# Delta-rule tiles of a two-block transformer in compact form: two 64-token chunks' diagonal blocks side by side, 64x64 products on quarters of the array

## The reference, cut to what matters

```
kb = k * beta[..., None]
lower = jnp.where(strict, jnp.einsum('bhncd,bhnsd->bhncs', kb, k) * decay, 0.0)
rhs = jnp.concatenate([v * beta[..., None], kb * jnp.exp(g)[..., None]], axis=-1)
sol = lax.linalg.triangular_solve(jnp.eye(C, dtype=jnp.float32) + lower, rhs,
                                  left_side=True, lower=True, unit_diagonal=True)
u, wk = sol[..., :Dv], sol[..., Dv:]
intra = jnp.where(incl, jnp.einsum('bhncd,bhnsd->bhncs', q, k) * decay, 0.0)
def step(S, inp):
    qc, kc, uc, wc, gc, ac = inp
    v_new = uc - jnp.einsum('bhck,bhkv->bhcv', wc, S)
    o = jnp.einsum('bhck,bhkv->bhcv', qc * jnp.exp(gc)[..., None], S) + jnp.einsum('bhcs,bhsv->bhcv', ac, v_new)
    S = S * jnp.exp(g_last)[..., None, None] + jnp.einsum(
        'bhck,bhcv->bhkv', kc * jnp.exp(g_last[..., None] - gc)[..., None], v_new)
```

## Time and profile before

| | us |
|---|---|
| median of 3 runs | 4289.7 (4287.04 to 4289.97) |
| the profiled execution | 4289.53 |
| its span in the trace | 4287.6 |
| PE, DVE, ACT, POOL busy | 3966.6, 1481.8, 1432.2, 1341.2 |
| mean granted TensorE clock | 0.935 of full speed |

### The profile page before, as it was taken

The page is one execution under the profiler, slowest core; times in us unless marked ns, Lnnn a source line. Parts: engine busy times, 40 slices in busy tenths (PEclk is TensorE's granted clock), DMA queues, the critical chain, the costliest instruction groups (busy, mean ns, idle before and its releaser), DMA issues.

```text
span 4287.6 us, 49148 instructions
## 1 busy us (share of the span) xinstructions
PE 3966.6 (93%) x20324; PEld 3286.1 (77%) x20324; DVE 1481.8 (35%) x3082; ACT 1432.2 (33%) x2399; POOL 1341.2 (31%) x639
## 2 busy tenths in 40 slices
PE   8988999998899979999988889999999998879999
PEld 7776888877688868877677778887887757778887
DVE  2344111334411231225855531112112686653111
ACT  2543222344322242234442232223223453313221
POOL 3203443410344444433200034443443320003443
PEclk9988999998899989999888899999999988889999
DMA  4102333210233333322100023333233210003232
GB/s 117 40 20 64 91 101 99 72 45 15 71 95 96 108 83 93 98 88 71 35 1 1 1 84 92 100 96 92 91 101 89 68 32 1 1 3 92 91 101 89
DMA packets 406767, 292.31 MB, mean 68 GB/s; under 512 B 18032, under 2 KB 356880, under 8 KB 406544
## 3 DMA queue, kind: packets, MB, share of 16 engines
q1 hardware_dynamic: 400976, 284.96, 22.4%
q10 hardware_dynamic: 5136, 2.96, 0.3%
q0 software_dynamic: 432, 1.25, 0.1%
HBM read 287.03 MB, written 2.10 MB: 67 GB/s over the span
## 4 chain that ended last, share of the span: by engine, by line
PE 54%; DVE 7%; ACT 2%; issue 1%; POOL 0%; ACTq 0%; DMA 0%; DVEq 0%; SPq 0%
PE ps L687 8%; PE ps L689 8%; PE ps L688 8%; PE ps L743 5%; PE ps L745 5%; PE ps L744 5%; PE ps L1264 1%; PE ps L1252 1%; PE ps L1271 1%; PE ps L789 1%; PE ps L1043 1%; PE ps L806 1%; DVE mix L1478 1%; PE ps L797 1%; PE ps L1354 1%
## 5 line engine op out<-in xcount | busy, mean ns | idle before, releaser
L2810 POOL TENSOR_TENSOR wl<-wraw,wh 128x1024 fp32r<-128x1024 f32 (+2 forms) x532 | 1248.0, 2347 | 2408.7 <-ACT wh L2242 2408.6
L687 PE MATMUL ps<-x_T,wh 128*128 128x512 f32 (+1 forms) x2672 | 1029.9, 385 | 33.4 <-DVE x_T L1443 23.7
L688 PE MATMUL ps<-x_T,wh 128*128 128x512 f32 (+1 forms) x2672 | 1022.6, 383 | 0.0
L689 PE MATMUL ps<-x_T,wl 128*128 128x512 f32 (+1 forms) x2672 | 1022.1, 383 | 0.0
L2242 ACT ACTIVATE wh<-wraw 128x1024 fp32r<-128x1024 f32 (+2 forms) x532 | 548.8, 1033 | 1149.7 <-PE ps L745 644.2
L687 PEld LDWEIGHTS ps<-x_T,wh 128*128 128x128 f32 x2672 | 512.1, 192 | 144.4 <-issue 48.4
L689 PEld LDWEIGHTS ps<-x_T,wl 128*128 128x128 f32 x2672 | 511.5, 191 | 95.9
L688 PEld LDWEIGHTS ps<-x_T,wh 128*128 128x128 f32 x2672 | 512.2, 192 | 93.8 <-issue 0.5
L743 PE MATMUL ps<-wh,h_T 128*128 128x512 f32 x1056 | 417.6, 395 | 27.4 <-issue 27.4
L745 PE MATMUL ps<-wh,h_T 128*128 128x512 f32 x1056 | 415.9, 394 | 0.0
L744 PE MATMUL ps<-wl,h_T 128*128 128x512 f32 x1056 | 415.8, 394 | 0.0
(11 more groups left out here) (812 smaller groups left out, 5214.8 us busy)
## 6 DMA issues: line engine op xcount, KB each, us to landing
wraw<-in_ffn_w_gate_dram SPq DMA_DIRECT2D x88, 512.0 KB, 3.8
wraw<-in_ffn_w_up_dram SPq DMA_DIRECT2D x88, 512.0 KB, 3.9
wraw<-in_w_in_dram SPq DMA_DIRECT2D x82, 512.0 KB, 3.8
wraw<-in_ffn_w_down_dram SPq DMA_DIRECT2D x80, 512.0 KB, 3.7
wraw<-in_w_gate_dram SPq DMA_DIRECT2D x44, 512.0 KB, 3.9
wraw<-in_w_up_dram SPq DMA_DIRECT2D x44, 512.0 KB, 3.9
wraw<-in_w_down_dram SPq DMA_DIRECT2D x40, 512.0 KB, 3.7
wraw<-in_w_o_dram SPq DMA_DIRECT2D x16, 512.0 KB, 3.4
```

The source lines that it names most:

```text
L687: mm(b[:, t0:t1], wh[:, k, :], xTh[:, k, t0:t1], k == 0, False)
L688: mm(b[:, t0:t1], wh[:, k, :], xTl[:, k, t0:t1], False, False)
L689: ins = mm(b[:, t0:t1], wl[:, k, :], xTh[:, k, t0:t1], False, k == 7)
L2810: tt(wl, raw_of(w), wh.bitcast(F32), ALU.subtract).then_inc(*g.sig("w", "lo", w))
```

## The change

Only the chunks' own 64x64 blocks are kept. The block of tokens 0 to 63 stands in partitions 0 to 63, the block of tokens 64 to 127 in partitions 64 to 127, over the same 64 columns. Four heads take 128x256, and both halves g share a buffer of 128x512: `Dm`, `Dt`, `N`, `Yk`. The products on them are 64x64x64, one for each chunk: the first reads rows 0 to 63 and writes PSUM partitions 0 to 63, the second rows 64 to 127 to partitions 64 to 127, of the same bank. The output is split: `od` holds what needs no state and is copied by ACT; the state's part `o` is added to Y by DVE. The masks become 64 columns wide.

```diff
+                def each(b, g, lhs, rhs):
+                    for h in range(4):
+                        for c in HALF:
+                            hs = slice(g * 256 + h * 64, g * 256 + h * 64 + 64)
+                            ins = mm(b[c, h * 64:(h + 1) * 64], lhs[c, hs], rhs[c, hs], True, True)
+                    return ins
...
-                        for h in range(4):
-                            hs = slice(h * P, (h + 1) * P)
-                            ins = mm(b[:, hs], N_[:, hs], D_[:, hs], True, True)
-                        ins.then_inc(*S("y", k, g))
+                        each(b, g, N, Dm).then_inc(*S("y", k, g))
...
-                    mm(b[:, 0:256], F2[hb(h), p_ * P:(p_ + 1) * P], fa, True, True)
-                    mm(b[:, 256:512], F2[hb(h), 256 + p_ * P:384 + p_ * P], fa, True,
-                       True).then_inc(*S("rw", h))
+                    for q in range(2):
+                        for n in range(2):
+                            for e_, c in enumerate(HALF):
+                                o = q * 256 + n * P
+                                ins = mm(b[c, o:o + P].rearrange("p (c n) -> p c n", c=2),
+                                         F2[rs, n * 256 + q * P + 64 * e_:n * 256 + q * P + 64 * e_ + 64],
+                                         f1v[rs, q, :, c], True, True)
...
-                for h in range(8):
-                    ins = mm(b[hb(h), (h // 2) * P:(h // 2 + 1) * P], KB[:, h * 64:(h + 1) * 64],
-                             (DR if h < 4 else DG)[:, (h % 4) * P:(h % 4 + 1) * P], True, True)
-                ins.then_inc(*S("wt"))
+                for e_, c in enumerate(HALF):
+                    b, free = bank(K("wt", e_), K("WT", e_))
+                    pe.wait_ge(*free)
+                    for h in range(8):
+                        ins = mm(b[hb(h), (h // 2) * 64:(h // 2 + 1) * 64], KB[c, h * 64:(h + 1) * 64],
+                                 Dm[c, h * 64:(h + 1) * 64], True, True)
+                    ins.then_inc(*S("wt", e_))
...
+                    ins.then_inc(*S("ubx", par))
...
-                        pe.wait_ge(*at(*K("WT")))
+                        pe.wait_ge(*at(*K("ubx", par)))
+                        pe.wait_ge(*at(*K("WT", e_)))
...
-                        if h < 4:
-                            mm(o, RW[h][:, 0:128], un, True, False)
-                            mm(o, RW[h][:, 256:384], VV[:, h * 64:(h + 1) * 64], False, False)
-                        else:
-                            mm(o, PN[par][:, (q - 2) * 256:(q - 2) * 256 + 128], un, True, False)
+                    for c in HALF:
+                        if h < 4:
+                            mm(b[c, hs], RW[h % 2][c, o:o + 64], UN[c, us], True, False)
+                        else:
+                            ins = mm(b[c, hs], PN[c, (h - 4) * P:(h - 4) * P + 64], UN[c, us], True, True)
...
-                        v.copy_predicated(v4(D_), lvm(k, 0).bitcast(I32), v4(psum_of(*K("d", k, g))[:, :])).then_inc(
-                            *S("D", k, g))
+                        v.copy_predicated(v4(D_), lvm(k, 0).bitcast(I32),
+                                          v4(psum_of(*K("d", k, g))[:, 0:256])).then_inc(*S("D", k, g))
...
-                for h in range(4):
-                    ins = tt(DR[:, h * P:(h + 1) * P], RW[h][:, 128:256], lvl(0), ALU.mult)
+                for par in range(2):
+                    ins = tt(Dm[:, 0:256].rearrange("p (q r n) -> p q r n", q=2, r=2)[:, :, par, :],
+                             RW[par].rearrange("p (q c n) -> p q c n", q=2, c=4)[:, :, 1, :], lvm(0, 0, 2), ALU.mult)
...
-                v.wait_ge(*at(*K("Y", 1)))
+                v.wait_ge(*at(*K("Y")))
+                for par in range(2):
+                    yp = Y.rearrange("p (q r n) -> p q r n", q=4, r=2)[:, :, par, :]
+                    v.wait_ge(*at(*K("o", par)))
+                    step(tt(yp, yp, v4(psum_of(*K("o", par))[:, 0:256]), ALU.add), *K("Yo", par))
```

More of the change, by code:

```diff
@@ L66, in make_consts @@
     same = (r // 64) == (c // 64)
+    r64, c64 = r % 64, np.arange(64)[None, :]
     lv = []
-    for k in range(6):
-        w = 1 << k
-        m = ((r // (2 * w)) == (c // (2 * w))) & ((r // w) % 2 == 0) & ((c // w) % 2 == 1)
-        lv.append(m.astype(f))
-    for k in range(6):
-        lv.append(lv[k].T.copy())
+    for tr in range(2):
+        for k in range(6):
+            w = 1 << k
+            a, b = (c64, r64) if tr else (r64, c64)
+            lv.append((((a // (2 * w)) == (b // (2 * w))) & ((a // w) % 2 == 0) & ((b // w) % 2 == 1)).astype(f))
+    lv += [(r64 <= c64).astype(f), (r64 < c64).astype(f), (r64 > c64).astype(f), (r64 == c64).astype(f)]
     ind = np.stack([(i < 64), (i >= 64)], 1).astype(f)
     c2 = np.concatenate(common + [rope_tab(32), (same & (r <= c)).astype(f), (same & (r < c)).astype(f),
-                                  (same & (r > c)).astype(f), ind] + lv[8:], 1)
-    r1, r2 = np.concatenate(masks + swa, 1), np.concatenate(lv[:8], 1)
-    assert c1.shape[1] == N1 and c2.shape[1] == N2 and r1.shape[1] == N3
+                                  (same & (r > c)).astype(f), ind], 1)
+    r1, r2 = np.concatenate(masks + swa, 1), np.concatenate(lv, 1)
+    assert c1.shape[1] == N1 and r2.shape[1] == N3 - R_X and c2.shape[1] == N2 and r1.shape[1] == N3
     return [np.ascontiguousarray(c_.astype(f)) for c_ in (c1, c2, r1, r2)]
@@ L1261, in rec_tile @@
                         pe.wait_ge(*at(*K("Dt", k - 1, g)))
-                        for h in range(4):
-                            hs = slice(h * P, (h + 1) * P)
-                            ins = mm(b[:, hs], Dt_[:, hs], y_[:, hs], True, True)
-                        ins.then_inc(*S("d", k, g))
+                        each(b, g, Dt, Yk).then_inc(*S("d", k, g))
                         if k < 5:
@@ L1268, in rec_tile @@
                             pe.wait_ge(*free)
[L1269 to L1273 removed]
+                            each(b, g, Yk, Dt).then_inc(*S("dt", k, g))
+                        if g:
+                            stock.put(pe, l, Yk)
                         yield
[L1275 removed]
+                stock.put(pe, l, Dt, N)
                 yield SOLVED
@@ L1335, in rec_tile @@
                 Y = get()
+                b, free = bank(K("od"), K("Y"))
+                pe.wait_ge(*free)
+                for h in range(8):
+                    hs, us = slice(h * 64, (h + 1) * 64), slice((h % 2) * 256 + (h // 2) * 64, (h % 2) * 256 + (h // 2) * 64 + 64)
+                    o = (h // 2) * 256
+                    for c in HALF:
+                        if h < 4:
+                            mm(b[c, hs], RW[h % 2][c, o:o + 64], UN[c, us], True, False)
+                        else:
+                            ins = mm(b[c, hs], PN[c, (h - 4) * P:(h - 4) * P + 64], UN[c, us], True, True)
+                    if h < 4:
+                        for c in HALF:
+                            mm(b[c, hs], RW[h % 2][c, o + P:o + P + 64], VV[c, hs], False, True)
@@ L2035, in rec_tile @@
                 yield
[L2036 to L2038 removed]
+                DTN = get()
+                RW = [get(), get()]
+                DT, DN = DTN[:, 0:256], DTN[:, 256:512]
                 v.wait_ge(*at(*K("gd")))
[L2040 to L2043 removed]
@@ L2689, in rec_tile @@
                 copy(X[:, 0:256], psum_of(*K("x"))[:, 0:256]).then_inc(*S("X"))
-                s.wait_ge(*at(*K("wt")))
-                copy(WT, psum_of(*K("wt"))[:, :]).then_inc(*S("WT"))
+                for e_ in range(2):
+                    s.wait_ge(*at(*K("wt", e_)))
+                    copy(WT[:, e_ * 256:e_ * 256 + 256], psum_of(*K("wt", e_))[:, 0:256]).then_inc(*S("WT", e_))
                 yield
@@ L2701, in rec_tile @@
                 Y = get()
-                for par in range(2):
-                    s.wait_ge(*at(*K("o", par)))
-                    copy(Y.rearrange("p (q r n) -> p q r n", q=4, r=2)[:, :, par, :],
-                         psum_of(*K("o", par))[:, 0:256].rearrange("p (q n) -> p q n", q=4)).then_inc(*S("Y", par))
-                stock.put(s, l, *RW, *PN, DR, DG, X, WT, K2, F1, F3)
+                s.wait_ge(*at(*K("od")))
+                copy(Y, psum_of(*K("od"))[:, :]).then_inc(*S("Y"))
+                stock.put(s, l, *RW, PN, Dm, X, WT, K2, F1, F3)
                 yield PASSED
```

257 lines of the change are left out of this document (117 added, 140 removed).

## The result

| | before | after |
|---|---|---|
| median of 4 runs | 4288.4 (4282.5 to 4290.0) | 4139.0 (4134.1 to 4140.1) |
| the profiled execution, its span | 4289.5, 4287.6 | 4140.1, 4138.2 |
| PE, DVE busy | 3966.6, 1481.8 | 3826.4, 1392.1 |
| mean granted clock | 0.935 | 0.926 |

The ratio is 0.9652, 95% interval 0.9635 to 0.9669: 149 us less, where the forecast was 51 less (4238, range 4140 to 4310). It is the first rival's number, 4130, that came within 9 us.

The account below looks back on a forecast made before the run. PE was taken to bind 38 us and DVE 34 us of a tile; half-clock terms gave -5.4 a tile, -43 for eight, and some 8 more for time at full clock: 4289.5 - 51 = 4238 us, range 4140 to 4310.

Parts of the forecast that it names:

- the first rival: Recurrence: the clock stays as high as before, -20 us a tile, -160 in all, 4130 us; chance 0.12.
- the five stretches: Parts of the third recurrence period, 71.8 us: PE sets three (38 us), DVE the other two (34 us).
- Quarter price: Solving products: one 64x64x64 record takes 0.054 us at half clock, a group of 16 takes 0.87.
- The third rival: Solving groups: a quarter record costs 0.066 us, +1.3 a tile, +10 for eight, 4300 us; chance 0.18.
- The full-clock sum: All stretches of a tile's period with the clock full throughout: -24.5 us a tile.
- A: First stretch, PE-bound (RW, N, four groups): 7.7 to 8.6 us at half clock, 4.5 at full.
- C: Third stretch, PE-bound (ub, state steps, d and dt, output): 22.1 to 19.1 us at half clock, -11 at full.
- D: Fourth stretch, 20.0 us, DVE-bound (masked copies, additions into Y): +0.4 us at half clock, -0.6 at full.
- E: Last stretch, 8.4 us, PE-bound (d and dt, eight transposes): -0.9 us at half clock, -3.8 at full.
- the low level for nearly all of the recurrence: Recurrence: granted clock near 0.50 to 0.60 with quarter work, giving -5.4 us a tile, -43 for eight.
- The 42 us row: Attention: clock at 0.50 through 42 us with PE busy 40.4, cited against the clock staying high.
- Rival 2: New groups: the two quarters don't overlap, 0.107 us a record, +21 a tile, +165, 4455 us; chance 0.10.

## Why the prediction was wrong, step by step

- **What bounds the kernel, the five stretches:** right. The same cuts describe the kernel after, with the same engine in each. (The second recurrence's slices are 34 to 36, counted as the first's 21 to 23 are, not 33 to 35; nothing hangs on it.)
- **Quarter price:** 0.054 us at half clock was taken; 0.059 measured, and 0.48 us a group at full clock where 0.44 was taken. Right within a tenth. The third rival (0.066) was wrong.
- **Masked copies and the D setup:** 0.43 taken and 0.44 measured; 3.2 taken and 3.0 measured. Right.
- **The output:** 4.3 us at half clock was the forecast, 2.2 at full; 2.1 measured at full.
- **The full-clock sum:** -24.5 a tile was worked out (47.3 us), and 48.4 measured. The arithmetic was good; it was put at the wrong level of the clock. That the total is so near is partly luck: A and C came out 0.7 and 1.5 us shorter than in this sum, D 0.9 and E 2.2 longer, the last two with the clock at 0.69.
- **The step that failed** is "I take the low level for nearly all of the recurrence". I had concluded that "full-array work is what went with the high level", from rows in which the clock was low under 64-column work, pairs on one half of the rows and attention. None of these rows showed a dense pair on both halves of the rows, which is nearly all that the change adds; I took them as the nearest. Measured are 0.86 and 0.82 in the second and third period, and 96 added records in such pairs raised the clock by themselves. What share of the 0.86 is the pairs' is not measured: quarter pairs in the old layout had 0.77 and 0.79. The 42 us row, said to speak against the first rival, spoke about attention and nothing else. Its chance of 0.12 was far too low; what the doubt deserved was an even split between two levels that lay 108 us apart.
- **The Trainium skill** (TensorE: Matmul & The Clock Gate, "Why this matters for your kernels") asks for a TensorE that stays continuously busy. By that rule the first rival was the forecast, and it came closer. But the rule is not the whole of it: in the kernel after PE is busy 90.3 of 92.2 us at 0.50, and of the 96 added records in 5.1 and in 5.4 us, PE busy in both, only those on both halves of the rows went with a rise.
- **The first tile** was costed at nothing ("the first tile's making lies among attention units whose DVE and ACT chains cover it"). It costs 6.5 us a layer, and up to 19 more were to be had there. Under the low clock PE is busy all the time there (50.0 of the 50 us from 2150 to 2200), so nothing covers. The row of the low stretch in the earlier trace rows ends at 2171, and I did not ask what the engine did between there and the rise at 2173.9: the full-array `gd` that the change takes out.
- **Rival 2, pairs in turn:** wrong twice over. They do not run in turn (0.030 us a record against 0.042 on one quarter, at full clock), and in turn they would have cost 0.042, not 0.054, and 37 us in all, not 165. The Trainium skill's sentence that different row tiles cannot access one bank at the same time (TensorEngine Tiling (Array Packing), "Gotcha 1: PSUM Pressure") does not hold here in that form: the two products of a pair write one bank, in different partitions, and follow each other at 0.030 us, sooner than two on the same quarter.
- **The rest of the sum:** eight tiles were counted as alike. They are not: two first ones lose 6.6 each, four gain 23, and two ends gain 33. 2 x 6.6 - 4 x 23 - 2 x 33 = -145. So the first rival, with eight times -20, had the right level of the clock and, by luck, the right total.

## What to carry to other kernels

Where the size of a change hangs on the level of TensorE's clock, work the sum out at both levels and ask of each row you quote whether it really has the work that the change brings; rows that lack it prove little. When a change takes full-array work out, look at what stood just before each rise of the clock in the trace; if it goes, the rise may go with it, and a few dummy products at the right place can be worth far more than they cost (53 us here with six; 11 us on the kernel before with twelve). In a chain that alternates between two engines, both engines' savings count nearly in full.

## What the runs showed of the hardware that was not expected

- Behind 96 records of 64x64x64 on diagonal quarters in turn (5.13 us) the granted clock rose from 0.50 to 1.00, as it did behind 24 full-array records of 256 columns (7.72 us); behind 96 on one half of the rows (5.38 us, half of them with zeros) and 72 on one quarter (7.94 us) it did not.
- At a granted clock of 0.50 PE can stay busy for 92 us without a rise, and in another execution the clock rose behind a burst of six full-array products; this took 53 us off the kernel. Six full-array records of the cumulative sums, in the same stretch, went with a rise in six profiles and with none in ten.
- A quarter record costs 0.030 us at full clock in diagonal pairs and 0.042 behind another on its own quarter. In the 36 products that all wrote the same place of PSUM it was 7.94 / 72 = 0.110 at half clock, which would be 0.055 at full (the expectation had 0.078 at half). Whether the common output or something else made them dearer wasn't tried.
